# The first modulation in two halves of features, with the first dense step started on the first half

## What is computed

```python
shm, scm, gm, shf, scf, gf = ada_mod(c, ada_w[l], ada_b[l])
cshm, cscm, cgm, cshf, cscf, cgf = ada_mod(c_ctx[None, :], ada_w[l], ada_b[l])
ux = modulate(rms_norm(h_x, norm_g[l, 0]), shm, scm)
uc = modulate(rms_norm(h_c, norm_g[l, 0]), cshm, cscm)
...
yx, yc = retention_mixer(ux, uc, ret_w_in[i], ret_w_out[i], ...)
```

## Time and profile before

| | |
|---|---|
| median of 3 runs | 1898.78 us (1897.29 to 1900.3) |
| profiled execution: time | 1900.46 us |
| its span | 1898.7 us |
| PE busy in the span | 95% |

### The profile page before, as it was taken

The page is one execution under the profiler, slowest core; times in us unless marked ns, Lnnn a source line. Parts: engine busy times, 40 slices in busy tenths (PEclk is TensorE's granted clock), DMA queues, the critical chain, the costliest instruction groups (busy, mean ns, idle before and its releaser), DMA issues.

```text
span 1898.7 us, 26235 instructions
## 1 busy us (share of the span) xinstructions
PE 1804.6 (95%) x9865; PEld 1505.9 (79%) x9865; DVE 1142.8 (60%) x1523; ACT 841.9 (44%) x1211; POOL 86.9 (5%) x164
## 2 busy tenths in 40 slices
PE   5999999999999999999989998899989988989997
PEld 3877767778688888888878886899889966779986
DVE  2766757666367688544356554666655674765554
ACT  3334243342456423233255554565555545554453
POOL 3000101101000111000000000000010000000000
PEclk8999999999999999999999998899999998999999
DMA  8644544545265466333213221455554443545662
GB/s 294 197 150 132 171 149 148 158 130 171 73 242 177 142 212 187 117 86 111 99 43 129 85 90 55 155 178 177 199 166 152 155 146 100 186 135 177 182 194 100
DMA packets 150910, 282.38 MB, mean 149 GB/s; under 512 B 12652, under 2 KB 78308, under 8 KB 150689
## 3 DMA queue, kind: packets, MB, share of 16 engines
q1 hardware_dynamic: 133344, 220.54, 36.3%
q0 software_dynamic: 17472, 60.57, 10.3%
HBM read 276.83 MB, written 4.23 MB: 148 GB/s over the span
## 4 chain that ended last, share of the span: by engine, by line
PE 83%; DVE 8%; ACT 5%; DMA 2%; issue 2%; POOL 0%; SPq 0%; ACTq 0%; DVEq 0%; POOLq 0%
PE ps L569 24%; PE ps L570 23%; PE ps L571 23%; PE ps L841 4%; DVE wl L2243 2%; PE ps L834 1%; ACT wh L1521 1%; DMA arena<-in_norm_g 1%; PE ps L705 1%; PE ps L1126 1%; DMA raw<-in_ada_w 1%; PE ps L1107 1%; PE ps L783 1%; PE ps L718 0%; PE ps L614 0%
## 5 line engine op out<-in xcount | busy, mean ns | idle before, releaser
L2243 DVE TENSOR_TENSOR wl<-raw,wh 128x1024 fp32r<-128x1024 f32 (+1 forms) x388 | 454.4, 1181 | 394.0 <-ACT wh L1521 391.2
L1521 ACT ACTIVATE wh<-raw 128x1024 fp32r<-128x1024 f32 (+1 forms) x388 | 393.0, 1022 | 620.9 <-PE ps L571 600.8
L569 PE MATMUL ps<-uh,wh 128*128 128x256 f32 (+1 forms) x1216 | 381.7, 314 | 7.3 <-DVE spare L2265 7.3
L569 PE MATMUL ps<-wh,uh 128*128 128x512 f32 (+2 forms) x960 | 369.2, 385 | 13.2 <-issue 8.9
L570 PE MATMUL ps<-ul,wh 128*128 128x256 f32 (+1 forms) x1216 | 379.8, 312 | 0.0
L571 PE MATMUL ps<-uh,wl 128*128 128x256 f32 (+1 forms) x1216 | 379.5, 312 | 0.0
L570 PE MATMUL ps<-wl,uh 128*128 128x512 f32 (+2 forms) x960 | 355.8, 371 | 0.0
L571 PE MATMUL ps<-wh,ul 128*128 128x512 f32 (+2 forms) x960 | 355.2, 370 | 0.0
L569 PEld LDWEIGHTS ps<-uh,wh 128*128 128x128 f32 x1216 | 233.5, 192 | 22.4 <-issue 7.0
L571 PEld LDWEIGHTS ps<-uh,wl 128*128 128x128 f32 x1216 | 233.6, 192 | 12.6
L570 PEld LDWEIGHTS ps<-ul,wh 128*128 128x128 f32 x1216 | 233.5, 192 | 12.4
(11 more groups left out here) (301 smaller groups left out, 1500.8 us busy)
## 6 DMA issues: line engine op xcount, KB each, us to landing
raw<-in_ffn_w_up SPq DMA_DIRECT2D x176, 256.0 KB
arena<-in_ada_w POOLq DMA_DIRECT2D x80, 512.0 KB, 4.1
raw<-in_w_in SPq DMA_DIRECT2D x60, 512.0 KB
raw<-in_ret_w_in SPq DMA_DIRECT2D x48, 512.0 KB
raw<-in_ffn_w_down SPq DMA_DIRECT2D x40, 512.0 KB
raw<-in_ret_w_out SPq DMA_DIRECT2D x32, 512.0 KB
raw<-in_w_up SPq DMA_DIRECT2D x32, 512.0 KB
raw<-in_w_down SPq DMA_DIRECT2D x32, 512.0 KB
```

Source lines behind the costliest of these rows:

```text
L569: pe.matmul(o, lh, rh, start=first, stop=False)
L1521: T.mark(act.activation(wh[:, j, 0:size], raw[:, j, 0:size], ACT.Copy), hi_done)
L2243: T.mark(vec.tensor_tensor(wl[:, j, 0:size], raw[:, j, 0:size], wh[:, j, 0:size], ALU.subtract), lo_done)
```

## The change

- Loads: the 16 units of the modulation no longer pass through `raw`. They go through eight buffers in the arena (`first`), and `raw` is free from the start for the units of step 0. The order of chunks is 0, 2, 1, 3 (`FIRST`), so that the first two chunks hold shift and scale of features 0 to 511, and the other two those of features 512 to 1023. SyncE issues chunks 0 and 2, the units 0 and 1 of step 0, chunks 1 and 3 (each load waits for the use of the buffer before), and units 2 and 3. Below, "chunk 1" to "chunk 3" of the changed kernel count in this new order.
- Norm: x and ctx are both transposed before step 0, and the transposed rows are kept unmodulated in the arena (`xt`) by ScalarE (even tiles) and VectorE (odd tiles). Scale and shift are applied in place from there, for both halves of the tokens together.
- TensorE: step 0 is one pass over all four token tiles (`dense_first`). Chunk 2 of the modulation stands behind the matmuls of unit 0, its turn and chunk 3 within those of unit 1, the last row turn and the table within those of unit 2.
- The scales are made in two halves (`first_scales`).
- GpSimdE's loads of decays and constants wait for the last of the 16 units instead of for the second split of step 0.
- PSUM banks of the rows' turns and of the modulation move from the `main` to the `side` half.

```diff
-        norm_a = (area(0, KD, SEQ), [area(8 + 4 * t, D) for t in range(4)])
+        rows_a, xt = [area(8 + 4 * t, D) for t in range(4)], area(24, KD, TOK)
+        first = [area(kb, UNIT) for kb in (0, 4, 40, 44, 54, 58, 71, 75)]
+        FIRST = (0, 2, 1, 3)
...
+            def load_first(n, u):
+
+                i = 4 * n + u
+                if i >= 8:
+                    sp.wait_ge(ada_used, i - 7)
+                v = a["ada_w"][0].rearrange("(j k p) n -> j p k n", k=2, p=P)
+                sp.dma_start(first[i % 8].rearrange("p (k n) -> p k n", k=2),
+                             v[u][:, :, FIRST[n] * 512:FIRST[n] * 512 + 512]).then_inc(first_loaded[i % 8], 16)
+
...
+            for half in range(2):
+                for n in (2 * half, 2 * half + 1):
+                    for u in range(SLOTS):
+                        load_first(n, u)
+                for j in (2 * half, 2 * half + 1):
+                    load_unit(part, j)
...
+            def dense_first(half):
+
+
+                G.next()
+                S.next()
+                for j in range(SLOTS):
+                    pe.wait_ge(lo_done, j + 1)
+                    pe.wait_ge(part_low, 2 * j + 2)
+                    for k in range(2):
+                        f = 2 * j + k
+                        for t in range(4):
+                            mm = three(ps[:, half + t, :], uh[:, f, t * P:(t + 1) * P], ul[:, f, t * P:(t + 1) * P],
+                                       wh[:, j, k * 512:(k + 1) * 512], wl[:, j, k * 512:(k + 1) * 512], f == 0, f == KD - 1)
+                        if k:
+                            mm.then_inc(unit_used, 1)
+                        yield j, k
+
+            for u in range(SLOTS):
+                first_ada(0, u)
+                if u == 2:
+                    turn_rows(2, 96, 2)
+            turn_part(0, rows_a[0:2], main)
             first_turn(0)
-            first_ada(1)
             turn_rows(1, 113, 9)
+            for u in range(SLOTS):
+                first_ada(1, u)
             first_turn(1)
-            first_ada(2)
-            turn_rows(3, 88, 2)
-            turn_rows(4, 88, 2)
...
+            turn_part(2, rows_a[2:4], main)
+            pe.wait_ge(xt_act, 2)
+            pe.wait_ge(xt_vec, 2)
+            for j, k in dense_first(main):
+                if (j, k) == (0, 1):
+                    for u in range(SLOTS):
+                        first_ada(2, u)
+                elif (j, k) == (1, 0):
+                    first_turn(2)
+                elif (j, k) == (1, 1):
+                    turn_rows(3, 88, 2)
+                    for u in range(SLOTS):
+                        first_ada(3, u)
+                    first_turn(3)
+                elif (j, k) == (2, 0):
+                    turn_rows(4, 88, 2)
+                elif (j, k) == (2, 1):
+                    turn_table()
...
+            squares(0)
+            keep_ada(0, side + 3)
+            squares(1)
+            keep_xt(0)
+            keep_ada(1, side + 2)
+            keep_xt(1)
             split(units=range(0, 1))
...
+            def apply_first(j):
+
+
+                f = 2 * j
+                for k in range(2):
+                    x = xt[:, f + 1, k * SEQ:(k + 1) * SEQ]
+                    T.mark(vec.tensor_scalar(x, x, acol[:, k, f + 1:f + 2], mcols(k, f + 1, 1), ALU.mult, ALU.add), part_odd)
+                split(units=range(j, j + 1))
+                T.settle()
+                for k in range(2):
+                    vec.wait_ge(part_hi, 2 * j + k + 1)
+                    o = slice(k * SEQ, (k + 1) * SEQ)
+                    T.mark(vec.tensor_tensor(ul[:, f:f + 2, o], xt[:, f:f + 2, o], uh[:, f:f + 2, o], ALU.subtract), part_low)
+
...
+            keep_xt(0)
+            for t in range(2, 4):
+                normalise_row(t, t, rows_a[t])
+            take_ada(1, side + 1)
+            first_scales(0)
+            keep_xt(1)
+            T.settle()
+            apply_first(0)
+            apply_first(1)
+            take_ada(2, side + 1)
             take_cols(fcol2[:, :], 88)
+            take_ada(3, side + 1)
+            first_scales(1)
+            apply_first(2)
             take_cols(fcol[:, 16:104], 88)
+            apply_first(3)
             group_full()
...
-            pool.wait_ge(lo_done, 2)
+            pool.wait_ge(ada_used, 16)
```

More of the change, by code:

```diff
@@ L352, in build @@
         raw_loaded = [sem(f"raw_loaded{j}") for j in range(SLOTS)]
+        first_loaded = [sem(f"first_loaded{j}") for j in range(8)]
+        xt_act, xt_vec = sem("xt_act"), sem("xt_vec")
         hi_done = sem("hi_done")
@@ L449, in load, with load_unit @@
                 for j in range(SLOTS):
[L451 to L457, removed]
+                    sp.wait_ge(lo_done, s * SLOTS + (j - SLOTS + 1))
+                    load_unit(parts, j)
+            def load_unit(parts, j):
+                pieces = parts(j)
+                for dst, src in pieces:
+                    sp.dma_start(dst, src).then_inc(raw_loaded[j], 32 // len(pieces))
             def cols(w, c0, n=512):
@@ L723, in _, with first_ada @@
             pe.wait_ge(pick_loaded, 16)
-            def first_ada(n):
-                if n > 1:
+            def first_ada(n, u):
+                if u == 0 and n > 1:
                     pe.wait_ge(ada_kept, n - 1)
[L729 to L733, removed]
+                i = 4 * n + u
+                pe.wait_ge(first_loaded[i % 8], 16 * (i // 8 + 1))
+                ada_matmuls(n, u, first[i % 8], side + 3 - n % 2)
             def first_turn(n):
@@ L752, in _ @@
[L752 to L758, removed]
+            pe.wait_ge(xt_act, 1)
+            pe.wait_ge(xt_vec, 1)
+            turn_part(2, rows_a[2:4], main)
[16 more added lines that the diff above has]
+                    turn_table()
@@ L864, in _ @@
                 d = 4 * h
-                dense = G.now()
-                if h == 0:
-                    pe.wait_ge(ada_kept, 4)
-                    pe.wait_ge(ada_taken, 4)
-                    for j in dense_tokens(main, ((0, 1), (2, 3)), fresh=1):
-                        if j == 2:
-                            pe.wait_ge(part_low, SLOTS)
-                            turn_part(2, norm_a[1][2:4], side)
-                else:
+                dense = G.now() if h else 6
+                if h:
                     mods_emptied(2 * h - 2)
@@ L1648, in _, with squares @@
             act.wait_ge(eps_set, 1)
-            for z in range(2):
+            def squares(z):
                 act.wait_ge((x_loaded, ctx_loaded)[z], 16)
@@ L2440, in log_sigmoid, with keep_xt, first_scales @@
                 T.mark(vec.scalar_tensor_tensor(out=lgt[:, 4, :], in0=q, scalar=-2.0, in1=s, op0=ALU.mult, op1=ALU.add), lg_ready)
+            def keep_xt(z):
+                vec.wait_ge(part_turned, z + 1)
+                T.mark(vec.tensor_copy(xt[:, 1:KD:2, z * SEQ:(z + 1) * SEQ],
+                                       ps[:, main + 2:main + 4, :].rearrange("p b (c n) -> p (b c) n", c=2)), xt_vec)
+            def first_scales(half):
+                T.settle()
+                for k in range(2):
+                    c = slice(4 * half, 4 * half + 4)
+                    T.mark(vec.scalar_tensor_tensor(out=acol[:, k, c], in0=mcols(k, 8, 8)[:, c], scalar=1.0,
+                                                    in1=gcol[:, c], op0=ALU.add, op1=ALU.mult), (vec_own, acol_ready)[k])
+                T.settle()
@@ L2453, in _ @@
             tick(emptied)
-            take_ada(2, main + 1)
-            for t in range(2, 4):
-                normalise_row(t, t, norm_a[1][t])
-            take_ada(3, main + 1)
-            scales(0, 8)
-            apply_part(0, side, norm_a[0], 0, 0, lambda j: split(units=range(j, j + 1)))
-            apply_part(1, side, norm_a[0], 1, 0)
             log_sigmoid()
```

109 lines of the change are left out of this document (60 added, 49 removed).

## The result

The changed kernel is slower: median 1905.2 us (1900.1 to 1908.61, 14 runs) against 1900.03 us (1897.29 to 1903.48, 14 runs) of the kernel before, a ratio of 1.0026 with a 95% interval of 1.0017 to 1.0034. The profiled execution took 1906.33 us, its span is 1904.5 us.

The account below looks back on a forecast made before the run. TensorE, busy 95%, was taken as the bound, so the start of step 1 counts: a 9.6 us lead, outweighed by moved work, waits and clock, gives +3.6 on 1898.8, thus 1902.4 us. Range: 1898.3 to 1906.3 us.

Parts of the forecast that it names:

- The lead: Opening: dense matmuls of step 0 start at 33.5 us instead of 43.10, 9.6 us earlier.
- Moved work: Within step 0: 6.8 us of modulation chunks, turns, rows and table that TensorE did before the step until now.
- The wait in the middle: Before unit 2 of step 0: TensorE waits 3.8 us, from 52.6 to 56.4, for scales, application and split.
- The clock: Half clock after rests: 1.7 us at the start of step 0, and 1.7 us more behind the wait before unit 2.
- The rival of a middle rest without a fall: Rest before unit 2 costs no clock: 1900.7 us, chance 0.18.
- The uncovered chain: At step 1: VectorE's 6.4 us chain for the decays ends late, so TensorE waits 1.7 us.
- the sum: Opening up to step 1: all terms added, step 1 at 70.4 us against 68.5, +1.9, or +3.6 with the clock.
- VectorE's lateness at the queries: Behind 80 us: new TensorE waits if VectorE, 2 us behind, does not catch up before the queries are turned; a wrong sign.
- One sign of being right: Behind the start of step 1, forecast at 70 to 74 us, nothing else changes.
- my own case: Whole kernel: the forecast of 1902.4 us, within 1901 to 1904, chance 0.33.
- a clock that is low early: Opening: first transposes do not bring the clock up in time, 1.4 to 3.4 us more, 1903.8 to 1905.8; chance 0.28.

Follow-up runs that it names:

- second trace: The changed kernel run again unaltered, against the kernel before on the same chip: 1903.63 us, ratio 1.0027.
- e3: Changed kernel with chunks 2 and 3 of the modulation, and the turn, earlier in step 0: 1898.81 us, ratio 0.9996 to the kernel before.
- e7: Changed kernel with 15 unread matmuls filling TensorE's wait before unit 2: 1901.9 us, ratio 1.0015 to the kernel before.
- e8: e5 with 21 unread matmuls behind the second transposes, in the wait before step 0: 1890.89 us, ratio 0.9955 to the kernel before.
- e5: Changed kernel with chunks earlier, rows and table ahead of unit 2, and decays behind unit 1: 1895.14 us, ratio 0.9979 to the kernel before.
- e1: Changed kernel with the last two row turns and the bias table ahead of chunk 3: 1902.41 us, ratio 1.0013 to the kernel before.
- e2: Changed kernel with the decays done behind unit 1 and their two loads issued at the start: 1901.75 us, ratio 1.0014 to the kernel before.
- e4: Changed kernel with 28 unread matmuls behind the turn of chunk 3, before unit 2: 1902.99 us, ratio 1.0012 to the kernel before.

## Why the prediction was right

**The lead.** 33.5 us was forecast and came at 32.75 (33.24 in the second trace). Most terms held to some tenths: transposes from 18.64, second transposes at full clock (1.94 instead of 1.75), no load late. Chunk 1 was through at 24.4 instead of 25.4; 0.4 of that is a slip of addition in the prediction, as 22.0, 0.58, 0.3 and twice 1.07 make 25.0. The two operations that no row of before showed cost 0.73 us for the two of VectorE (0.6 taken) and 1.09 for the two of ScalarE (0.9 taken).

**Moved work.** 2.1 us a chunk was taken, 1.93 measured.

**The wait in the middle.** 3.8 was forecast, 3.85 and 3.86 came. `e3` shows that its place does it: with chunk 3 ahead of unit 1 it is 0.95.

**The clock.** +1.7 was taken for the restart in the middle; `e7` gives 1.4. At the start of step 0 I took 1.7 as well; there it was 2.9 in this trace (24 matmuls in 8.4 us instead of 5.5), since half clock lasted longer behind the restart. The rival of a middle rest without a fall did not come in any trace of this order. The Trainium skill's section on bursts with waits between them (TensorE: Matmul & The Clock Gate, "HAM oscillation — how this bites in real kernels") is borne out by the two traces of the changed kernel: both restarts were paid. `e8` has neither and starts step 1 first, 0.9 us ahead of `e5`, which pays the one at the start.

**The uncovered chain.** 1.7 was forecast, 1.17 came. The clock is not the reason: `e7`, whose unit 2 runs at full clock, waits 1.15. From the row turn within unit 2 to the first matmul of step 1 the sum had 11.3 us (59.1 to 70.4), and 10.8 passed (60.39 to 71.22): VectorE's ticks, taken as 0.25 and 0.2 us, left gaps of under 0.05 us between the operations about them. `e1` and `e2` each remove it, so it is both the row turn ahead and the decays behind unit 3 that make it.

**What was not in the sum.** The 0.76 us at the second unit of step 1. TensorE waits there until VectorE has rotated the result of step 0. In the trace of before this ended 0.6 us ahead of TensorE's need (73.35 against 73.9 us), and a VectorE that is 4.2 us late can't be in time when TensorE is only 2.8 late. The prediction looked for VectorE's lateness at the queries, one unit later, where there was slack. With it the sum would have been 1903.2. One sign of being right, that nothing else changes behind step 1, did not hold for this reason.

**Near the right value for partly balancing reasons.** Terms: start 0.75 earlier, restart at the start 1.2 dearer, chain 0.5 cheaper, second unit 0.76 not seen. At the first matmul of step 1 the shift was +2.7 us, 0.9 below the forecast +3.6; the wait that was not in the sum brought it to +3.8 one unit later. That the opening came so near is luck in these terms, and the mechanism is what was right. The medians differ by 5.2 us, and by 4.6 in the second comparison; the 0.3 to 1.4 us beyond the two openings are not explained by them. The median, 1905.2 us, lies in the stated range, but above the 1901 to 1904 of my own case and among the times that I gave to a clock that is low early. That rival's mechanism is in neither trace of the changed kernel (chunk 1 took 1.93 us in both); whether it came in executions without a trace is not known. Behind 600 us the two traces of the changed kernel part by 3.4 us, by a wait for VectorE and by stretches at half clock; whether this averages out between two kernels was not tried.

## What to carry to other kernels

- Starting a dependent product on half of its inputs splits one exposed chain (reduce, turn, scale, apply) into two. Here it paid only when the second chain ran under matmuls (`e3`, `e5`): issue its inputs' work one piece ahead of the last piece that can cover it, not right before the product that needs it.
- When an engine with an in-order queue gets work behind a later event, look at everything that stands behind it there: a 0.25 us copy that waited for a row turn moved a 6.4 us chain and the splits of the next step into the open. Price the lag at each following meeting of the two engines, not at the first alone.
- In an opening of short bursts, fill a wait of known length with matmuls that nobody reads, cut to less than the wait: it brought step 1 forward by 1.4 us in `e7` and 0.9 in `e8`. Measure one of them first: the 28 of `e4` outlasted the wait, and step 1 came 1.2 us later.

## What the runs showed of the hardware

- A matmul of an fp32 identity with itself, 128 x 128, is two instructions here and takes 0.23 us at full clock (28 in 6.50 us, 15 in 3.59, 21 in 4.85).
- How long half clock lasts behind the same restart differs from trace to trace. In `e1_rows_early` and `e2_decays_early` TensorE's code up to the end of unit 0 is the same, the rest ahead is 5.4 us and the first dense matmul starts at 33.28 and 33.27 us; the first 24 took 7.0 and 8.5 us.
- The operations on 256 columns from SBUF are dear for their size: 0.41 us each on VectorE where 1024 columns took 0.75.
